# Turning the pooling input weights on VectorE in 32x32 blocks, from four loads per tile, in place of TensorE transposes

## The reference, cut to what matters

```
h = x @ w_in
u, z = split(h)                          # 2048 columns each
p = pooled(u) - u                        # along the sequence, group by group
m = einsum('btgc,gcd->btgd', p, w_grp) + b_grp
y = m * scale * silu(z);  out = y @ w_out
```

## Time and profile before

| what | value |
|---|---|
| runs | 1911.58, 1911.59, 1911.77 us; median 1911.59 |
| span of the profiled execution, first to last instruction | 1908.1 us |
| its own time | not listed apart; the three runs lie within 0.2 us, so 3.5 us lie around the span |
| TensorE (PE) busy, whole span | 1856.8 us, 97% |
| `prepare`: first product to last | 9.15 us to 124.92 us |
| DMA, whole span | 351 MB, 184 GB/s on average |

### The profile page before, as it was taken

How to read it: one execution, slowest core, us unless ns; L and a number is a source line. 1 busy time by engine, 2 the same in 40 slices (tenths; PEclk the granted TensorE clock), 3 DMA queues, 4 the chain that set the end, 5 groups by cost and what they waited for, 6 DMA issues and landing times.

```text
span 1908.1 us, 24512 instructions
## 1 busy us (share of the span) xinstructions
PE 1856.8 (97%) x8680; PEld 1526.4 (80%) x8680; DVE 1383.8 (73%) x1715; ACT 858.4 (45%) x1316; POOL 658.9 (35%) x460
## 2 busy tenths in 40 slices
PE   8989999999999899999989999999999999999997
PEld 7778886887788788888768888887888887887885
DVE  3455556779676787777696777758899978446997
ACT  4554335656655543444444444444434444224231
POOL 1323323232231000143545565405577534223330
PEclk9999999999999899999999999999999999999998
DMA  8966665439354945666724444242545436647442
GB/s 279 316 215 240 212 192 204 134 101 303 82 162 116 354 152 171 224 229 227 267 103 162 137 159 151 84 170 88 181 173 192 162 106 253 216 164 264 174 146 99
DMA packets 266629, 351.22 MB, mean 184 GB/s; under 512 B 19344, under 2 KB 193168, under 8 KB 261904
## 3 DMA queue, kind: packets, MB, share of 16 engines
q1 hardware_dynamic: 263824, 342.36, 53.7%
q0 software_dynamic: 2688, 7.34, 1.1%
HBM read 225.92 MB, written 123.73 MB: 183 GB/s over the span
## 4 chain that ended last, share of the span: by engine, by line
PE 55%; DVE 6%; issue 3%; DMA 2%; ACT 1%; POOL 1%; SPq 0%; DVEq 0%; ACTq 0%; POOLq 0%
PE banks L202 16%; PE banks L204 16%; PE banks L203 16%; DVE m_w_lo L2714 2%; PE banks L1720 1%; PE banks L1725 1%; DVE m_x_lo L2728 1%; DMA m_x_raw<-w_terms 1%; PE banks L1704 1%; PE banks L1702 1%; ACT m_x_hi L2534 1%; DMA v<-v_tiles 1%; DMA m_ahead<-x_terms 0%; DVE m_win_a L2747 0%; PE banks L2457 0%
## 5 line engine op out<-in xcount | busy, mean ns | idle before, releaser
L202 PE MATMUL banks<-m_x_hi,m_w_hi 128*128 128x512 f32 x1312 | 515.0, 393 | 9.5 <-DVE m_z L2789 4.6
L204 PE MATMUL banks<-m_x_hi,m_w_lo 128*128 128x512 f32 x1312 | 513.4, 391 | 0.0
L203 PE MATMUL banks<-m_x_lo,m_w_hi 128*128 128x512 f32 x1312 | 512.9, 391 | 0.0
L202 PEld LDWEIGHTS banks<-m_x_hi,m_w_hi 128*128 128x128 f32 x1312 | 247.1, 188 | 66.2 <-issue 7.6
L203 PEld LDWEIGHTS banks<-m_x_lo,m_w_hi 128*128 128x128 f32 x1312 | 246.9, 188 | 53.3 <-issue 0.7
L204 PEld LDWEIGHTS banks<-m_x_hi,m_w_lo 128*128 128x128 f32 x1312 | 246.8, 188 | 52.6
L202 PE MATMUL banks<-b_hi,h_w_hi 128*128 128x512 f32 x656 | 258.0, 393 | 4.5 <-issue 3.5
L204 PE MATMUL banks<-b_hi,h_w_lo 128*128 128x512 f32 x656 | 256.4, 391 | 0.0
L203 PE MATMUL banks<-b_lo,h_w_hi 128*128 128x512 f32 x656 | 256.0, 390 | 0.0
L2521 ACT ACTIVATE m_w_hi<-m_s 128x512 fp32r<-128x512 f32 x182 | 114.3, 629 | 204.8 <-PE banks L204 179.5
L2714 DVE TENSOR_TENSOR m_w_lo<-m_s,m_w_hi 128x512 fp32r<-128x512 f32 x182 | 162.5, 897 | 32.8 <-ACT m_w_hi L2521 31.7
(11 more groups left out here) (277 smaller groups left out, 3450.1 us busy)
## 6 DMA issues: line engine op xcount, KB each, us to landing
b_raw<-x_in SPq DMA_DIRECT2D x14, 1024.0 KB, 9.7
m_x_raw<-x_terms SPq DMA_DIRECT2D x9, 1024.0 KB, 7.7
p_in<-in_pool_w_in SPq DMA_DIRECT2D x32, 256.0 KB, 5.4
w_fused<-p_out SPq DMA_DIRECT2D x32, 256.0 KB, 3.8
x_in<-h_terms SPq DMA_DIRECT2D x8, 1024.0 KB, 4.3
v_tiles<-h_v_out SPq DMA_DIRECT2D x16, 512.0 KB, 5.1
in_raw<-in_gla_w_in SPq DMA_DIRECT2D x16, 512.0 KB, 5.4
h_raw<-in_gla_w_in SPq DMA_DIRECT2D x16, 512.0 KB, 5.9
```

Source lines behind the costliest of these rows:

```text
L202: nc.tensor.matmul(out, a_hi, b_hi, start=first, stop=False, skip_group_check=True)
L203: nc.tensor.matmul(out, a_hi, b_lo, start=False, stop=False, skip_group_check=True)
L204: return nc.tensor.matmul(out, a_lo, b_hi, start=False, stop=last, skip_group_check=True)
```

## The change

It takes the four TensorE transposes of a tile away and turns the tile on VectorE, which transposes each 32x32 block in its own 32 partitions. Blocks have to be in the right 32 partitions beforehand, so each tile is loaded by four DMAs: load `q` brings the 128 channels `q*128 ..` of all 128 rows into partitions `32q .. 32q+31`, as four runs of 512 B per partition (64 KB, 32 partitions). After the turn, partition `32q + j` of slice `t` holds channel `128q + 32t + j`, so the contraction goes over the channels in another order, and the rows of the group weights are loaded in that same order, also by four DMAs of 32 partitions (256 KB each, runs of 2 KB). The product is the same sum.

The turned tile goes to a new SBUF buffer `p_t_raw` (two of them), from which ScalarE and VectorE make `hi` and `lo`; before, they read PSUM. VectorE's order at tile `n` becomes: `lo(n)`, turn `n+2` (after the four loads of that tile), the quarter's `lo`, `b_lo`; tiles 0 and 1 are turned ahead of the loop. The group weights have one semaphore for all four loads, and a group's loads wait for all four `lo` of the one before; those of group 0 are issued by ScalarE instead of SyncE.

```diff
-        src_in = a["pool_w_in"][0].rearrange("(k p) c -> k p c", p=P)
+        src_in = a["pool_w_in"][0].rearrange("(k b i) c -> k i b c", b=QUADS, i=SQUARE)
-        src_grp = a["pool_w_grp"][0].rearrange("g (k p) c -> p g k c", p=P)
+        src_grp = a["pool_w_grp"][0].rearrange("g (q t j) c -> g q j t c", q=QUADS, j=SQUARE)
...
                 def load_in(n):
                     if n >= IN:
                         sp.wait_ge(turned, n - IN + 1)
-                    sp.dma_start(w_in[n % IN][:], src_in[n % KT, :, n // KT * GW:(n // KT + 1) * GW]
-                                 ).then_inc(in_loaded[n % IN], DMA)
+                    for q in range(QUADS):
+                        first = n // KT * GW + q * P
+                        sp.dma_start(w_in[n % IN][q * SQUARE:(q + 1) * SQUARE, :].rearrange("i (b c) -> i b c", c=P),
+                                     src_in[n % KT, :, :, first:first + P]).then_inc(in_loaded[n % IN], DMA)
...
                 def load_grp(g):
-                    for c in range(GT):
-                        if g:
-                            sp.wait_ge(g_lo, (g - 1) * GT + c + 1)
-                        sp.dma_start(w_grp[:, c, :], src_grp[:, g, c, :]).then_inc(grp_loaded[c], DMA)
+                    sp.wait_ge(g_lo, g * GT)
+                    for q in range(QUADS):
+                        sp.dma_start(w_grp[q * SQUARE:(q + 1) * SQUARE, :, :], src_grp[g, q]).then_inc(grp_loaded, DMA)
...
-                load_in(0)
-                load_grp(0)
-                for n in range(1, IN - 1):
+                for n in range(IN - 1):
                     load_in(n)
...
             @block.tensor
-                turn(0)
                 for n in range(TILES):
-                    if n + 1 < TILES:
-                        turn(n + 1)
...
             @block.scalar
+                for q in range(QUADS):
+                    act.dma_start(w_grp[q * SQUARE:(q + 1) * SQUARE, :, :], src_grp[0, q]).then_inc(grp_loaded, DMA)
                 for n in range(TILES):
                     act.wait_ge(turned, n + 1)
-                    nc.scalar.activation(t_hi[n % 2][:].rearrange("p c d -> p (c d)"), turned_ps[n % 2],
-                                         ACT.Copy).then_inc(hi, 1)
+                    nc.scalar.activation(t_hi[n % 2][:], t_raw[n % 2][:], ACT.Copy).then_inc(hi, 1)
...
             @block.vector
+                def turn(n):
+                    dve.wait_ge(in_loaded[n % IN], (n // IN + 1) * QUADS * DMA)
+                    nc.vector.transpose(t_raw[n % 2][:].rearrange("p t (b i) -> p b t i", i=SQUARE),
+                                        w_in[n % IN][:].rearrange("p (b t j) -> p b t j", b=QUADS, j=SQUARE)
+                                        ).then_inc(turned, 1)
+                for n in range(2):
+                    turn(n)
                 for n in range(TILES):
                     dve.wait_ge(hi, n + 1)
-                    nc.vector.tensor_tensor(t_lo[n % 2][:].rearrange("p c d -> p (c d)"), turned_ps[n % 2],
-                                            t_hi[n % 2][:].rearrange("p c d -> p (c d)").bitcast(F32),
-                                            ALU.subtract).then_inc(lo, 1)
+                    nc.vector.tensor_tensor(t_lo[n % 2][:], t_raw[n % 2][:], t_hi[n % 2][:].bitcast(F32), ALU.subtract
+                                            ).then_inc(lo, 1)
+                    if n + 2 < TILES:
+                        dve.wait_ge(lo, n + 1)
+                        turn(n + 2)
```

More of the change, by code:

```diff
@@ L217, in prepare @@
     PAIR_AT = 23
+    SQUARE = 32
+    QUADS = P // SQUARE
     OUT_LAG = 2
@@ L227, in prepare @@
     grp_lo = [p.place(f"p_grp_lo{s}", [P, GT, GW], F32R) for s in range(2)]
+    t_raw = [p.place(f"p_t_raw{s}", [P, GT, P]) for s in range(2)]
     t_hi = [p.place(f"p_t_hi{s}", [P, GT, P], F32R) for s in range(2)]
@@ L240, in prepare @@
         stored = p.fused_stored
-        grp_loaded = [sem(f"grp_loaded{c}") for c in range(GT)]
+        grp_loaded = sem("grp_loaded")
         b_loaded = {j: sem(f"b_loaded{j}") for j in V_LOADS}
@@ L246, in prepare @@
                              "pool_done", "ones_in", "w_summed", "b_summed", "b_hi_done"))
-        src_in = a["pool_w_in"][0].rearrange("(k p) c -> k p c", p=P)
+        src_in = a["pool_w_in"][0].rearrange("(k b i) c -> k i b c", b=QUADS, i=SQUARE)
         v_src = a["gla_w_in"][0].rearrange("(k p) c -> p k c", p=P)
-        src_grp = a["pool_w_grp"][0].rearrange("g (k p) c -> p g k c", p=P)
-        turned_ps = [p.ps[:, s, :] for s in range(2)]
+        src_grp = a["pool_w_grp"][0].rearrange("g (q t j) c -> g q j t c", q=QUADS, j=SQUARE)
         out_ps = [p.ps[:, 2 + s, :] for s in range(2)]
@@ L388, in _ @@
             def _(pe):
[L389 to L396, removed]
                 def turn_x(t):
@@ L434, in grp_part @@
                 def grp_part(g, c):
-                    act.wait_ge(grp_loaded[c], (g + 1) * DMA)
+                    act.wait_ge(grp_loaded, (g + 1) * QUADS * DMA)
                     if g >= 2:
```

## The result

The changed kernel took 1921.64 us in the median (1920.86 to 1922.21) where the kernel before took 1911.63 on the same chip: ratio 1.0057, 95% interval [1.0045, 1.0069], 10.0 us slower. Its profiled execution took 1921.79 us, with a span of 1920.0 (1908.1 before).

The account below looks back on a forecast made before the run. It took PE as the bound in tiles 1 to 5, PE and DMA both full in 6 to 17, PE again ahead in 18 to 31; +1.3 - 2.4 - 0.3 - 5.2 = -6.6 us gave 1905.0 us, range 1898 to 1914.

Parts of the forecast that it names:

- Start: Before the first product: it needs three tiles, twelve issues, so it starts at 10.5 us instead of 9.15, +1.3 us.
- VectorE's turn: Every tile: the transpose on VectorE takes 0.7 us and hides in a product's 2.72 us, except at x tiles.
- the x tile's chain: Tiles 18 to 31: from the turn of x to the next tile's product, 4.96 us, which stays.
- Tiles 1 to 5: First stretch of prepare: PE-bound, TensorE's turns go, 14.4 us against 16.84, -2.4 us.
- Tiles 6 to 17: Middle stretch: DMA sets it and PE's saving goes into waiting, 42.3 us against 42.6, -0.3 us.
- the bounds of the 32-partition load: Middle stretch, tile loads: 329 GB/s, +1.8 us, to 202 GB/s, +7.8 us; the forecast stayed at the lower end.
- rival (a): Tile loads of 32 partitions move at half rate: +7.8 in place of +1.8, 1911.0 us, no change; chance 0.24.
- the tiles' term: Middle stretch, cost of loading tiles into 32 partitions: +1.8 us taken, about +9 by the skill's page.
- SyncE's queue: Load and store issues per tile, middle stretch: 2.9 us against 3.5 us a tile, fitting with little room.
- rival (b): SyncE's queue takes over from a mean issue of 0.62 us: +10.3, 1921.9 us, slower; chance 0.13.
- Tiles 18 to 31: Last stretch: x tiles keep 4.96 us, other tiles shrink to 2.72; 44.8 us against 50.0, -5.2 us.

Follow-up runs that it names:

- f1_grpfull: The changed kernel with group weights loaded on all 128 partitions (row 4p+t to partition p), a semaphore per piece; ratio 1.0043 to the kernel before.
- f3_cols: f1_grpfull with each tile loaded by four loads of 128 columns on 128 partitions, blocks not put in place; ratio 1.0023 to the kernel before.
- f4_plain: f1_grpfull with one plain load per tile, runs of 2 KB, blocks not put in place; ratio 0.9997 to the kernel before.
- g1_quiet: f4_plain with GpSimd's four sums for the next block replaced by fills with zero; ratio 0.9982 to the kernel before.
- f: Four runs of the changed kernel with group weights on 128 partitions, differing in semaphores or tile loads; ratios 1.0043, 1.0043, 1.0023 and 0.9997.
- g2: f4_plain with the first two 1 MB loads issued at tiles 3 and 5 in place of 6 and 8; ratio 0.9993 to the kernel before.
- h: Three runs: one 512 B-run load per tile; VectorE's turn in the last group alone; that with GpSimd's sums held back; ratios 1.0003, 0.9983, 0.9983.

## Why the prediction was wrong

It forecast 1905.0 us, faster; the kernel took 1921.6, slower, outside the range of 1898 to 1914.

*Start (+1.3; measured +4.5).* The order was right: three tiles, then `lo` of the group. The terms add up to 10.7 (5.9 + 3.5 + 0.7 + 0.7), not 10.5, which changes little. What failed is "lands near 9.3 with the same 3.5 us", for the third tile: even the first was turned only at 9.64 us, and the second at 10.93 (rows of `f1_grpfull` above). The loads share DMA with 1 MB of group weights, and the first 9.2 us moved 165 GB/s at a share of 0.86. With the group weights on 128 partitions it is 187 GB/s and a first turn at 8.28 us (`f1_grpfull`), with the tiles on 128 as well 232 and 7.06 (`f3_cols`), with one load per tile 247 and 5.59, and the first product at 10.34, +1.2 (`f4_plain`). So the form of the tiles' loads has the larger share of it, and the group weights' the smaller one, for which the prediction had no price. That 10.34 is close to the forecast is in part luck: it needs three issues and not twelve.

*VectorE's turn (0.7 us; measured 0.71).* Profile after, groups of DVE (busy us, mean ns, idle before):
```profile
L465 DVE STREAM_TRANSPOSE p_t_raw<-p_in 128x512 f32<-128x512 f32 x32 | 22.8, 712 | 49.5 <-DMA p_in<-in_pool_w_in 48.9
```
Right, and it is not the bound; it waits 48.9 us for its tiles. But "that happens only where GpSimd works, in the middle stretch" was wrong: GpSimd also forms the next block's sums in the last one (its 5.08 us stand in the earlier trace rows), on the x tile's chain, for 2.9 us in `f4_plain`.

*Tiles 1 to 5 (-2.4; measured -1.1).* The tile without a stall takes 2.72 us as said, and `f4_plain` needs 14.8 for the stretch, forecast 14.4. After, DMA's share is 1.06 there in place of 0.64, and the product at 25.29 us waits 0.79 us for `p_t_lo`: the loss of rate reaches this stretch too, which the prediction had left out of it.

*Tiles 6 to 17 (-0.3; measured +11.9).* The step that failed is the choice between the bounds of the 32-partition load, with no term at all for the group weights, which are loaded in the same way. I took the lower end because the nearest row had the same source and the same run; that row had all 128 partitions. Against rival (a) I also held that only three tenths of the bytes were `p_in`'s; by the earlier trace rows it is less, 13 loads of 0.262 MB out of 15.06, but the group weights belong with them. The runs put the 32 partitions of both at 6.5 us (after against `f3_cols`), about the 6.0 by which (a) raised the sum; that is partly chance, since (a) counted the tiles of the middle stretch alone. That the tiles have 3.8 us of it and the group weights 2.7 is less sure than the sum. With the dear loads gone the stretch took 44.2 us against the 42.3 forecast, so the rest of the step (DMA is full, PE's saving goes into waiting) fits. By the rule of the Trainium skill's page "SBUF — State Buffer" (Door 1: The DMA port swizzle), which the prediction cited and set aside, the tiles' term was to be about +9, an estimate; the runs agree that there is a cost, and put it at 3.8 us for the tiles.

*SyncE's queue (2.9 of 3.5 us; "nearly all issues take 0.4 to 0.5").* Before, the mean of the tile loads in that stretch was already 0.59. After, it was 0.65, past the 0.62 from which rival (b) was to decide, and the queue's slack fell from 68.8 to 5.2 us. But (b)'s sign was gaps in DMA, and DMA was full (1.03). Its 1921.9 us were 0.3 from the result, by a coincidence: of the 11.5 us of the loads' form four issues are 3.8 and the 32 partitions 6.5, and (b)'s +1.3, +7.2 and +1.8 stand against +4.5, +11.9 and +0.1.

*Tiles 18 to 31 (-5.2; measured +0.1).* The x tile's chain was right: 4.96 us in `f4_plain` (87.76 to 92.72), as forecast. But two waits stood outside it. The middle's lag reached into tiles 17 to 21 (16.0 us in `f4_plain`, 13.7 before), and GpSimd's sums held up tile 25. Where neither acts, as in `g1_quiet` from tile 21 on, four tiles took 13.5 us in place of 14.6 and 15.1: 2.7 us of gain, some half of what I had forecast for the stretch.

So of 15.6 us of TensorE time that the change frees, 3.6 us were to be had in tiles 1 to 9 (`f4_plain`) and 2.7 at the end. With plain loads the steps from tile 9 to 21 gave back 5.6 (48.3 us in place of 42.7): some 2.5 of it is the clock (below), and how the rest divides between full DMA and the order of the waits isn't shown. GpSimd took most of what the end had to give. The loads' form cost 11.5 us more (1.0057 against 0.9997).

## What to carry to other kernels

A busy engine is worth relieving only in the stretches where the next resource has room: read DMA's share and GB/s for each stretch, and SyncE's waits as its slack, before counting the saved instructions. A rearrangement that is left to the loads is paid in DMA's rate: count the partitions that each transfer fills, its outermost dimension, and its issues, for every tensor that is loaded so, and take the dear end of a bound when the full stretch has no room for it. An operand moved from PSUM to SBUF can make an instruction wait for another engine (0.68 us before, 1.75 beside GpSimd here); look for GpSimd in every stretch, not only where it is busiest.

## What I had not expected of the hardware

*The clock after a wait.* Before, TensorE kept its full clock in all three stretches (1.00 in the earlier trace rows). After the change it was granted 0.87 in the middle stretch, and `f4_plain` shows where. Timeline of PE, `f4_plain`, and its busy time by stretch:
```profile
50.57 0.77 PE L202 MATMUL banks<-p_grp_hi,p_t_hi 128*128 128x512 f32 x1 [4.54 <-ACT p_out L419]
51.13 0.63 PE L203 MATMUL banks<-p_grp_lo,p_t_hi 128*128 128x512 f32 x1
51.56 0.63 PE L204 MATMUL banks<-p_grp_hi,p_t_lo 128*128 128x512 f32 x1
```
```profile
50.60:55.80 5.20, 5.20 (x12) 4.07 (x13) 3.94 (x5) 1.97 (x4) 0.00 (x0) 0.50 0.92 278
```
After a wait of 4.54 us, matmuls start 0.43 us apart, not 2.72 / 12 = 0.23: the granted clock is half there (0.50), 1.2 in place of 2.4 GHz, and the tile takes 5.26 us (the next one starts at 55.83). So this wait cost more than its length: some 2.5 us on top of 4.5.

*The stride of VectorE's turn.* The block transpose took 0.71 us with adjacent columns and 1.10 with every fourth (rows of DVE above), which the `f`, `g1`, `g2` and `h` runs carry. Behind an x tile it costs nothing that shows: the product waits 1.19 us with either (in `g1_quiet` above, and in the timeline of PE after, at 133.53). Ahead of the first product it does, 0.8 us for two turns in a row (rows of `f1_grpfull` above), so that what `f1_grpfull` and the runs after it gain on the change can come out that much too small.
